# Seven half-size products in place of eight for three more chunks of an input projection (two of keys, one of values), with all sums on VectorE

## What is computed

```python
z = h @ p['in_w']
zq, zk, zv, za, zb, zg, hv, h1, h2, hg = split_cols(z, EVEN_SPLITS)
...
qkv = jax.nn.silu(depthwise_conv(jnp.concatenate([zq, zk, zv], axis=-1), conv_w).astype(jnp.float32))
q, k, v = split_cols(qkv, (GDN_QK_W, GDN_QK_W, GDN_W))
q = l2_normalize(q.reshape(B, L, GDN_HEADS, GDN_DK))
k = l2_normalize(k.reshape(B, L, GDN_HEADS, GDN_DK))
```

## Time and profile before

| | before |
|---|---|
| device time, median of 3 runs | 1008.84 us (1008.42 to 1009.04) |
| the profiled execution, its device time | 1007.34 us |
| its span, first to last instruction | 1005.5 us |
| TensorE busy | 984.0 us (98%) |
| VectorE busy | 588.5 us (59%) |
| ScalarE busy | 298.5 us (30%) |
| GpSimd busy | 120.3 us (12%) |
| TensorE's share of the chain that ended last | 93% |
| mean granted TensorE clock | 0.991 of full speed |

### The profile page before, as it was taken

The page is one execution under the profiler, slowest core; times in us unless marked ns, Lnnn a source line. Parts: engine busy times, 40 slices in busy tenths (PEclk is TensorE's granted clock), DMA queues, the critical chain, the costliest instruction groups (busy, mean ns, idle before and its releaser), DMA issues.

```text
span 1005.5 us, 13384 instructions
## 1 busy us (share of the span) xinstructions
PE 984.0 (98%) x5211; PEld 721.1 (72%) x5211; DVE 588.5 (59%) x1242; ACT 298.5 (30%) x780; POOL 120.3 (12%) x169
## 2 busy tenths in 40 slices
PE   6999999999999999999999999999999999999997
PEld 2447667554665566979999888888999755556786
DVE  3657555998965489885387233431757565453113
ACT  3053110201122345532202134114311565444111
POOL 4010000030300152100232110200000300010001
PEclk8999999999999999899999999999999999999999
DMA  8743441130220200112148204720502100000102
GB/s 257 275 133 119 140 154 44 40 84 0 68 78 34 84 1 1 42 44 63 43 142 277 86 1 126 233 74 0 168 4 81 57 1 1 0 2 1 42 1 105
DMA packets 68422, 78.10 MB, mean 78 GB/s; under 512 B 2700, under 2 KB 64135, under 8 KB 68360
## 3 DMA queue, kind: packets, MB, share of 16 engines
q1 hardware_dynamic: 64258, 68.96, 21.9%
q0 software_dynamic: 2432, 7.56, 2.3%
q10 hardware_dynamic: 1669, 0.72, 0.3%
HBM read 73.74 MB, written 3.51 MB: 77 GB/s over the span
## 4 chain that ended last, share of the span: by engine, by line
PE 93%; DVE 3%; DMA 2%; ACT 1%; SPq 1%; issue 0%; POOLq 0%; POOL 0%; DVEq 0%; ACTq 0%
PE ps L1398 83%; PE ps L1617 5%; PE ps L1428 2%; DMA wring<-in_mod_w 2%; PE ps L2017 1%; ACT phase L1331 1%; DVE phase L2326 1%; PE ps L1533 0%; PE ps L1438 0%; ACT phase L1334 0%; PE ps L1801 0%; DVE phase L2328 0%; DVE phase L2949 0%; SPq L631 0%; DVE wring L2555 0%
## 5 line engine op out<-in xcount | busy, mean ns | idle before, releaser
L1398 PE MATMUL ps<-hT,wring 128*128 128x128 f32 (+4 forms) x1088 | 261.7, 399 | 0.0
L1398 PEld LDWEIGHTS ps<-hT,wring 128*128 128x128 f32 x1088 | 162.5, 191 | 96.0 <-issue 89.6
L1398 PE MATMUL ps<-phase 128*128 128x256 f32 (+4 forms) x760 | 207.1, 420 | 3.7 <-DVE mix L2959 1.3
L1398 PEld LDWEIGHTS ps<-phase 128*128 128x128 f32 (+1 forms) x760 | 128.7, 191 | 71.4 <-issue 51.1
L1398 PE MATMUL ps<-wring,mix 128*128 128x256 f32 x560 | 122.1, 379 | 0.8 <-DVE mix L2957 0.8
L1398 PEld LDWEIGHTS ps<-wring,mix 128*128 128x128 f32 x560 | 105.9, 190 | 15.8 <-DVE mix L2957 1.6
L1398 PE MATMUL ps<-phase,hT 128*128 128x256 f32 (+3 forms) x336 | 78.8, 391 | 0.8 <-ACT phase L1376 0.8
L1398 PEld LDWEIGHTS ps<-phase,hT 128*128 128x128 f32 x336 | 60.5, 190 | 16.6 <-issue 11.4
L1398 PE MATMUL ps<-hT,phase 128*128 128x64 f32 (+4 forms) x276 | 55.8, 345 | 0.0
L1617 PE MATMUL ps<-ident,phase 128*128 128x128 f32 x400 | 50.0, 279 | 0.5 <-ACT phase L1334 0.4
L1617 PEld LDWEIGHTS ps<-ident,phase 128*128 128x128 f32 x400 | 46.4, 144 | 5.3 <-issue 4.0
(11 more groups left out here) (390 smaller groups left out, 1278.6 us busy)
## 6 DMA issues: line engine op xcount, KB each, us to landing
wring<-in_mod_w SPq DMA_DIRECT2D x18, 1024.0 KB, 5.2
wring<-in_even_in_w SPq DMA_DIRECT2D x16, 1024.0 KB, 5.8
phase<-in_mod_w SPq DMA_DIRECT2D x6, 1024.0 KB, 5.2
wring<-in_odd_in_w SPq DMA_DIRECT2D x5, 1024.0 KB, 9.0
phase<-in_odd_in_w SPq DMA_DIRECT2D x4, 1024.0 KB, 10.4
wring<-in_odd_out_w SPq DMA_DIRECT2D x4, 1024.0 KB, 5.3
wring<-in_even_out_w SPq DMA_DIRECT2D x3, 1024.0 KB, 10.2
xreg<-in_x_sample SPq DMA_DIRECT2D x1, 2048.0 KB, 16.9
```

The source lines that it names most:

```text
L1398: return nc.tensor.matmul(o, l, r, start=first, stop=last)
```

## The change

The chunks k0, k1 and v0 take the way of seven products too. Their three fills become seven each (21 fills for 9). The sums S1 to S4 are made once more, into `key_mixed`, since the first ones were overwritten; each of the three chunks has its own T sums (`key_wsum`), and the seven additions use three buffers of their own (`key_temps`). ScalarE no longer copies the three chunks to `pad`; it copies X alone. The core of the diff:

```diff
-       ("in_q0", 3), ("fft1_back", 5), ("in_q1", 3), ("in_k0", 3), ("cumsum", 1), ("tr_q", NT), ("in_k1", 3), ("in_v0", 3), ("tr_k", NT),
+       ("in_q0", 3), ("fft1_back", 5), ("in_q1", 3), ("in_k0", 7), ("cumsum", 1), ("tr_q", NT), ("in_k1", 7), ("in_v0", 7), ("tr_k", NT),
...
+        even_temps = [even_first, even_second, even_third]
+        key_mixed = [view(12800 + 4 * HALF * n, 4, HALF) for n in range(4)]
+        key_wsum = [[view(at + 512 * n, 4, P) for n in range(4)] for at in (17920, 20992, 5120)]
+        key_temps = [view(19968 + HALF * n, HALF) for n in range(3)]
...
+        KEYS = (2, 3, 4)
+        hyena_f, keys_f = [hy_rows[n] for n in SEVEN], [qkv_f[j] for j in KEYS]
...
             take_rows(qkv_f[1], 7)
             silu_rows(qT, cm[:, 0, :, :], 12)
-            take_rows(qkv_f[2], 8)
+            copy_even_first(qkv_f[2], key_temps, None)
             act.wait_ge(scal_ready, 1)
...
             take_turned(start["tr_q"], q_tm)
-            take_rows(qkv_f[3], 9)
+            copy_even_first(qkv_f[3], key_temps, qkv_f[2])
             silu_rows(kT, cm[:, 1, :, :], 16)
-            take_rows(qkv_f[4], 10)
+            copy_even_first(qkv_f[4], key_temps, qkv_f[3])
             take_turned(start["tr_k"], k_tm)
...
                 even_product(X, B11, A11)
...
-                pe.wait_ge(even_mixed_ready, 4)
-                pe.wait_ge(even_wsum_ready, 4 * (n - SEVEN[0]) + 4)
+                pe.wait_ge(sums_ready, 4)
+                pe.wait_ge(wsums_ready, 4 * n + 4)
                 even_product(W, T2, S2)
...
+            def project_keys(n):
+
+                project_seven(keys_f[n], key_mixed, key_mixed_ready, key_wsum[n], key_wsum_ready, n)
...
             project_qkv(1)
-            project_qkv(2)
+            project_keys(0)
...
             turn_cm(start["tr_q"], qT, 4, toks)
-            project_qkv(3)
-            project_qkv(4)
+            project_keys(1)
+            project_keys(2)
...
             dve.wait_ge(hy_done, 5)
+            dve.wait_ge(Y_ready, 6)
...
             tt(gsm[:, T1, :, :], gsm[:, T0, :, :], gsm[:, T1, :, :], ALU.min).then_inc(g_chain, 1)
+            tt(S1, A21, A22, ALU.add).then_inc(key_mixed_ready, 1)
+            tt(S3, A11, A21, ALU.subtract).then_inc(key_mixed_ready, 1)
...
             chained(nc.vector.reciprocal(gsm[:, BE, :, :], gsm[:, BE, :, :]))
+            dve.wait_ge(key_mixed_ready, 1)
+            tt(S2, S1, A11, ALU.subtract).then_inc(key_mixed_ready, 1)
+            dve.wait_ge(key_mixed_ready, 3)
+            tt(S4, A12, S2, ALU.subtract).then_inc(key_mixed_ready, 1)
+
+            def sum_key_chunk(n):
+
+                B11, B12, B21, B22 = even_quarters(keys_f[n])
+                T1, T2, T3, T4 = key_wsum[n]
+                wait_chunk(dve, chunk_of[keys_f[n] + 6])
+                tt(T3, B22, B12, ALU.subtract).then_inc(key_wsum_ready, 1)
+                tt(T1, B12, B11, ALU.subtract).then_inc(key_wsum_ready, 1)
+                dve.wait_ge(key_wsum_ready, 4 * n + 2)
+                tt(T2, B22, T1, ALU.subtract).then_inc(key_wsum_ready, 1)
+                dve.wait_ge(key_wsum_ready, 4 * n + 3)
+                tt(T4, B21, T2, ALU.subtract).then_inc(key_wsum_ready, 1)
+
+            def add_keys(n):
+
+                add_even_middle(keys_f[n], key_temps)
+                add_even_last(keys_f[n], key_temps)
...
             convolve_qkv(0)
+            sum_key_chunk(0)
             convolve_qkv(1)
+            sum_key_chunk(1)
+            add_keys(0)
             convolve_qkv(2)
+            sum_key_chunk(2)
             f = start["cumsum"]
             wait_full(dve, f)
...
             tt(gsm[:, KDF, :, :], gsm[:, TOT, :, :], gsm[:, CS, :, :], ALU.subtract).then_inc(scal_ready, 1)
+            add_keys(1)
             convolve_qkv(3)
             sum_heads(0)
+            add_keys(2)
             convolve_qkv(4)
```

More of the change, by code:

```diff
@@ L579, in chunk_list @@
             for j, f in enumerate(qkv_f):
-                lst.append((even, (Q0, K0, V0)[j // 2] + WC * (j % 2), WC, f + 2))
+                lst.append((even, (Q0, K0, V0)[j // 2] + WC * (j % 2), WC, f + (6 if j in KEYS else 2)))
             lst.append((even, ZG0 + WC, WC, start["in_z1"] + 2))
@@ L1014, in take_turned, with copy_even_first @@
                     nc.scalar.activation(dst[:, t, :], bank(f0 + t), ACT.Copy).then_inc(free(f0 + t), 1)
-            def copy_even_first(n):
-                f = hy_rows[n]
+            def copy_even_first(f, temps, before):
                 wait_full(act, f)
-                if n > SEVEN[0]:
-                    wait_drained(act, hy_rows[n - 1] + 5)
-                nc.scalar.activation(even_first, bank(f)[:, 0:HALF], ACT.Copy).then_inc(free(f), 1)
+                if before is not None:
+                    wait_drained(act, before + 5)
+                nc.scalar.activation(temps[0], bank(f)[:, 0:HALF], ACT.Copy).then_inc(free(f), 1)
             for n in range(5):
                 if n in SEVEN:
-                    copy_even_first(n)
+                    copy_even_first(hy_rows[n], even_temps, hy_rows[n - 1] if n > SEVEN[0] else None)
                     for which in LATE[2 * n:2 * n + 2]:
@@ L1583, in even_product, with project_seven @@
                 ins.then_inc(full(f), 1)
-            def project_seven(n):
-                wait_chunk(pe, chunk_of[hy_last[n]])
-                X, W, V, Z, V2, X2, Z2 = [hy_rows[n] + i for i in range(7)]
+            def project_seven(f, mixed_rows, sums_ready, wsums, wsums_ready, n, pair=()):
+                wait_chunk(pe, chunk_of[f + 6])
+                X, W, V, Z, V2, X2, Z2 = [f + i for i in range(7)]
                 A11, A12, A21, A22 = [hT[:, 4 * k:4 * k + 4, HALF * r:HALF * r + HALF] for r in range(2) for k in range(2)]
-                B11, B12, B21, B22 = even_quarters(n)
-                T1, T2, T3, T4 = even_wsum
-                S1, S2, S3, S4 = even_mixed
+                B11, B12, B21, B22 = even_quarters(f)
+                T1, T2, T3, T4 = wsums
+                S1, S2, S3, S4 = mixed_rows
                 even_product(X, B11, A11)
@@ L2309, in convolve @@
             def convolve(f, width, w0, b0, dst, m0, parts=(0, 1)):
-                if f in [hy_rows[n] for n in SEVEN]:
+                if f in hyena_f + keys_f:
                     for last in (f + 4, f + 5, f + 6):
@@ L2368, in add_rows, with add_even_middle, add_even_last @@
                 ins.then_inc(signal, 1)
[L2370 to L2372 removed]
+            def add_even_middle(f, temps):
+                X, W, V, Z, V2, X2, Z2 = [f + i for i in range(7)]
+                first_, second_, third_ = temps
                 wait_drained(dve, X)
                 wait_full(dve, W)
[L2375 removed]
+                tt(second_, bank(W)[:, 0:HALF], first_, ALU.add).then_inc(free(W), 1)
                 wait_drained(dve, W)
                 wait_full(dve, V)
[L2378 removed]
+                tt(third_, bank(V)[:, 0:HALF], second_, ALU.add).then_inc(free(V), 1)
                 wait_drained(dve, V)
                 wait_full(dve, Z)
[L2381 to L2382 removed]
+                add_rows(Z, 1, 1, third_, even_middle_ready)
+                tt(second_, bank(Z)[:, 0:HALF], second_, ALU.add).then_inc(free(Z), 1)
                 wait_full(dve, V2)
[L2384 to L2388 removed]
+                add_rows(V2, 1, 0, third_, free(V2))
+            def add_even_last(f, temps):
+                X, W, V, Z, V2, X2, Z2 = [f + i for i in range(7)]
+                first_, second_, third_ = temps
                 wait_full(dve, X2)
[L2390 removed]
+                add_rows(X2, 0, 0, first_, free(X2))
                 wait_drained(dve, Z)
                 wait_full(dve, Z2)
[L2393 removed]
+                add_rows(Z2, 0, 1, second_, free(Z2))
             sum_even_rows()
@@ L2495, in _ @@
                         .then_inc(hy_done, 1)
+            A11, A12, A21, A22 = [hT[:, 4 * k:4 * k + 4, HALF * r:HALF * r + HALF] for r in range(2) for k in range(2)]
+            S1, S2, S3, S4 = key_mixed
             dve.wait_ge(hy_done, 5)
+            dve.wait_ge(Y_ready, 6)
             chained(tt(gsm[:, T0, :, :], ab[:, :, 0:8], dtb.unsqueeze(1).broadcast_to([P, NT, 8]), ALU.add))
```

24 lines of the change are left out of this document (14 added, 10 removed).

## The result

| | before | changed |
|---|---|---|
| device time, median of 6 runs each | 1008.63 us (1007.08 to 1009.20) | 1012.26 us (1010.63 to 1013.22) |
| ratio to before | | 1.0037, 95% interval 1.0024 to 1.0050 |
| the profiled execution, its device time | 1007.34 us | 1012.48 us |
| its span | 1005.5 us | 1010.5 us |
| mean granted TensorE clock | 0.991 | 0.986 |

The change makes the kernel slower by 3.6 us at the median. The forecast was 2.0 us, at 1010.9; 1012.26 lies inside the range of 1007.0 to 1013.0.

The account below looks back on a forecast made before the run. TensorE, busy 98% of the span, was taken as the bound. -6.7 saved + 1.4 and 5.8 of waits + 1.5 of clock = +2.0 us on the 1008.84 median, or 1010.9 us; range 1007.0 to 1013.0.

Parts of the forecast that it names:

- The saving on TensorE: Chunks k0, k1 and v0: seven products each instead of three fills save TensorE 6.7 us in all.
- The first wait: Before product W of k0: TensorE waits 1.4 us for VectorE's T sums of k0.
- The second wait: Before product V of k1: TensorE waits 5.8 us until VectorE has copied cumsum out of V's bank.
- The clock behind it: Behind the wait before V of k1: granted clock falls to 0.50, costing 1.5 us, ends 0 and 3.4.
- The sum for the stage: From q1 to tr_k: saving, two waits and lowered clock, -6.7 + 1.4 + 5.8 + 1.5 = +2.0 us.
- Everything behind the stage: From tr_k to the end: only the stage's lateness carries on, with the same clock fall near 415; nothing added.
- rival C: Slow clock lasts longer, behind the new wait (1.9 more) or at the inverses (some 1.7 more): 1012.7 us, chance 0.2.
- Rival B: At the first inverse step the old clock fall does not come, returning 3.4 us: 1007.4 us, chance 0.2.
- Rival A: Copies of cumsum are not late, only the wait before W of k0 remains: -5.3, 1003.5 us, chance 0.05.
- the first wait's clock: Behind the wait before W of k0: a clock fall there was taken to cost 0, upper end 2 us.
- the prediction had warned of with S1 and S3: VectorE before 287.38: S1 and S3 fill an idle 3.48 us waiting for ScalarE; uncovered they would cost 2.9 us.

Follow-up runs that it names:

- e9: Changed kernel with cumsum copies right behind k0's additions, k0's T sums ahead of q0's convolution, k1's between q0's and q1's convolutions: 1002.84 us.
- e1: Changed kernel with VectorE's copies of cumsum moved ahead of k0's convolution and v0's T sums: 1003.84 us, ratio 0.9954 to before.
- e2: Changed kernel with the T sums of k0 moved ahead of q0's convolution: 1013.55 us, ratio 1.0054 to before.
- e8: Changed kernel with only v0's T sums moved behind the copies of cumsum, k0's convolution staying ahead: 1006.75 us, ratio 0.9986 to before.
- e3: Changed kernel with six unread matmuls of 512 columns put ahead of product W of k1: 1009.27 us, ratio 1.0001 to before.
- e5: Kernel before, with one unread matmul of 512 columns where TensorE waits for the first inverse step: 1008.55 us, ratio 0.9998 to before.

## Why the prediction was right, and where it was not

- **The saving on TensorE, 6.7 us.** Right. v0 took 15.07 us (predicted 15.08), and with the waits nearly gone the stage shrank by 5.8 us (e9), by 5.2 with one of them left (e1).
- **The first wait, 1.4 us.** Right: W began 303.92 - 283.01 = 20.91 us into the stage, where the sum of q1 and X gives 19.46, so 1.45; e2 shows that it hung on the T sums.
- **The second wait, 5.8 us.** Right in place and cause, a little too long: W was ready at 319.72 + 4.31 = 324.03, V began at 329.53, so 5.50. VectorE's additions with their overlaps took 318.12 - 314.73 = 3.39 us for the 3.5 assumed. e1 and e8 show the cause: the wait goes with the copies' place in VectorE's queue and shortens by what is taken from ahead of them.
- **The clock behind it, 1.5 us.** The mechanism was right, the size too small. The five products from 329.53 to 342.38 took 12.85 us for 10.77, so 2.1 us, and e3 gives 2.0. The row from which the 1.5 came was misread, too. The wait of 4.29 us before 24.21 did not lower the clock, which was low already before that wait began, at about 19.9; it had fallen during the wait of 2.46 us ahead of the run at 17.99:

```profile
16.00:18.00 2.00, 0.01 (x2) 0.81 1.10 349
18.00:20.00 2.00, 1.92 (x16) 0.50 1.12 364
```

  So the 1.5 had no row that bore it, and that it came within 0.6 us is partly luck.
- **The sum for the stage.** -6.7 + 1.45 + 5.5 + 2.1 = +2.35 for a measured +2.41, where the forecast had +2.0.
- **Everything behind the stage, 0 us.** This is the term that was mis-sized: the rest grew by 1.3 us. The forecast had it only as rival C, "or after the old one, which would then lose some 1.7 more", with a chance of 0.2 together with a longer stretch at the new wait. That half of C came, in both profiles. With it the two known differences are 2.4 + 1.3 = 3.7 us, beside the 3.6 between the medians.
- **Rival B, -3.4 us if the old fall were spared.** The fall came, and the price was too high. I priced the slow stretch at half its length, as if TensorE alone set the pace there. e5 kept the clock up over the first matmuls behind the wait and nothing came back, as VectorE's convolution was just as late. Only the transposes behind it could have gained, 3.54 us for the 1.91 that 16 such records take at full clock (at 403.80 in e5), so some 1.6 us by my estimate. That is less than the +2.0, so B could not have made the kernel faster. In e5 the clock was low again under them, so no run shows these 1.6. The +1.7 of rival C has the same flaw in the other direction: only what the slow stretch adds beyond that cover counts, and 1.3 was seen (1.4 at the place itself, 69.72 - 68.29).
- **Rival A.** It did not come by itself, since every piece of VectorE's path lasted as its row said. Its time, 1003.5 us, is what e1 reached by changing the order (1003.84).
- **That the first wait's clock would not matter.** Its clock stayed up: k0's remaining products, 303.92 to 316.92, took 13.00 us for 12.92.
- **In e2 I failed** for the reason that the prediction had warned of with S1 and S3: I moved sums out of a gap without asking what that gap had been.

What stays open is what sets the moment at which the clock falls at the inverses, and with it whether it stays low for 6.8 us or for 10.2. Both kernels that were profiled twice were the same both times, but two profiles of each don't show whether that holds in every execution.

## What to carry to other kernels

When a chunk's result is spread over more PSUM fills, every bank comes round sooner: look which short read-out now guards a bank that the next big step needs, and put that read-out at the head of its engine's queue. Here 0.4 us of copies behind 11 us of other work turned a gain of nearly 5 us into a loss of 3.6. Sums that look free may be filling a gap that another engine makes, so move something else into it when they go. And before a slow stretch of the clock is priced, ask how much of it another engine, late at the same place, already hides.

## What the runs showed of the hardware that was not expected

- A wait of 2.68 us of TensorE between float32 matmuls of 320 columns left the granted clock at 1.00 (e8), while some 1.12 us between matmuls of 64 columns lowered it to 0.50 in all nine profiles without a filler there (before and changed twice each, e1, e2, e3, e8 and e9, the wait being 1.12 or 1.13 us). In the kernel before a wait of 2.46 us for a weight load, after short bursts of matmuls with waits between them, saw it fall at about 17.2 us. The length of a wait alone does not tell whether the clock falls.
- After the wait of 5.34 us the clock was low for 4.2 us of work, and it had gone down during the wait, so only part of the slow stretch cost time: 2.0 us. After 7.25 us (e2) it was low for longer, with 0.60 on average over the next seven.
- The start of q1 moved by up to 2.4 us between kernels whose TensorE program up to there is the same, about as much as the effects studied here: 1.2 us of it was the landing of the second weight load (24.14 in e1, 25.31 in e9), the rest the low clock behind it (until 27.4 and 31.2). Stages cut from the timeline repeated within 0.15 us.
